# Hybrid trunk, one core: weights of four units split again in the second half, transfers issued one a slot, score groups in pairs

## The reference, cut to what matters

```
h = rmsnorm(x, g_pre[l]) * (1.0 + scale[:, None]) + shift[:, None]
p = h @ w_in[l]                       # 2048 x 1024 by 1024 x 8704
(a_in, a_g, b_q, b_f, b_i, b_g, c_x, c_b, c_c, c_g,
 d_q, d_k, d_v, d_g, m_g) = jnp.split(p, IN_OFFSETS, axis=-1)
y_pool = pool_mixer(a_in, ...) * silu(a_g)
y_hgrn = hgrn2_mixer(b_q, b_f, b_i, ...) * silu(b_g)      # gated linear recurrence
y_conv = short_conv_mixer(c_x, c_b, c_c, ...) * silu(c_g)
y_diff = diff_attention(d_q, d_k, d_v, ...) * silu(d_g)   # causal, two softmax maps a head
merged = sum over branches of sigmoid(m_g) * (y_branch @ w_merge_branch)
x = x + gate[:, None] * rmsnorm(merged @ w_out[l], g_post[l])
```

## Time and profile before

| | us |
|---|---|
| median of 3 runs | 2409.23 (2408.41 to 2409.46) |
| the profiled execution | 2409.45 |
| its span, first to last instruction | 2407.7 |
| TensorE busy | 2245.6 |
| VectorE, ScalarE, GpSimd busy | 1474.8, 1122.4, 847.1 |
| moved by DMA | 569.99 MB |
| mean granted TensorE clock | 0.972 |

### The profile page before, as it was taken

One profiled execution on the slowest core, in us unless ns is written; L12 is line 12 of the kernel. 1 busy time (PEld: TensorE's weight loads), 2 busy tenths in 40 slices (PEclk: granted clock), 3 DMA queues, 4 the chain that ended last, 5 costly groups with the idle time before them and its releaser, 6 DMA issues. The chain is left out here.

```text
span 2407.7 us, 35100 instructions
## 1 busy us (share of the span) xinstructions
PE 2245.6 (93%) x11573; PEld 1857.7 (77%) x11573; DVE 1474.8 (61%) x2645; ACT 1122.4 (47%) x2388; POOL 847.1 (35%) x739
## 2 busy tenths in 40 slices
PE   3798999998999999898999999999999978899998
PEld 3586788887777778786888888878888856787886
DVE  7766777748888795314776666445555435375571
ACT  5543566635454444323656665433434334344351
POOL 1223333326565563101222223133424306363453
PEclk7898999999999999999999999999999989999999
DMA  7899888678877778988565665587877775465561
GB/s 266 297 355 354 285 252 263 233 252 300 271 247 264 253 246 275 345 254 265 160 189 171 171 179 159 169 277 234 248 238 251 219 259 225 146 231 194 186 227 61
DMA packets 340780, 569.99 MB, mean 237 GB/s; under 512 B 27360, under 2 KB 213120, under 8 KB 335744
## 3 DMA queue, kind: packets, MB, share of 16 engines
q1 hardware_dynamic: 306336, 443.04, 54.7%
q10 hardware_dynamic: 34272, 124.80, 16.6%
HBM read 336.53 MB, written 236.45 MB: 238 GB/s over the span
## 5 line engine op out<-in xcount | busy, mean ns | idle before, releaser
L1772 PE MATMUL gb<-h_hi,w_both 128*128 128x512 f32 x1904 | 784.5, 412 | 71.4 <-DVE o L1308 34.1
L1774 PE MATMUL gb<-h_hi,w_both 128*128 128x512 f32 x1904 | 753.8, 396 | 0.0
L1773 PE MATMUL gb<-h_lo,w_both 128*128 128x512 f32 x1904 | 751.6, 395 | 0.0
L1772 PEld LDWEIGHTS gb<-h_hi,w_both 128*128 128x128 f32 x1904 | 363.8, 191 | 155.8 <-issue 79.8
L1774 PEld LDWEIGHTS gb<-h_hi,w_both 128*128 128x128 f32 x1904 | 362.7, 191 | 80.4
L1773 PEld LDWEIGHTS gb<-h_lo,w_both 128*128 128x128 f32 x1904 | 364.9, 192 | 66.2
L999 ACT ACTIVATE o<-gb 128x512 f32<-128x512 f32 x272 | 161.7, 594 | 381.8 <-PE gb L1774 324.8
L863 POOL TENSOR_TENSOR C_prob<-C_prob,C_cf 128x512 f32<-128x512 f32 (+3 forms) x160 | 159.6, 1022 | 464.3 <-DVE C_cf L1416 460.0
L1064 ACT ACTIVATE C_prob<-C_sc,C_negm 128x512 f32<-128x512 f32 (+3 forms) x320 | 198.4, 622 | 223.0 <-DVE C_negm L1394 215.3
L1308 DVE TENSOR_TENSOR o<-gb,o 128x512 f32<-128x512 f32 x204 | 140.2, 688 | 225.8 <-PE gb L1774 205.2
L1298 DVE TENSOR_TENSOR w_both<-w,w_both 128x512 fp32r<-128x512 f32 x170 | 153.3, 902 | 109.8 <-ACT w_both L976 109.6
(11 more groups left out here) (239 smaller groups left out, 3745.0 us busy)
## 6 DMA issues: line engine op xcount, KB each, us to landing
wS_scratch<-w_both SPq DMA_DIRECT2D x238, 512.0 KB, 3.9
w_both<-wS_scratch ACTq DMA_DIRECT2D x238, 512.0 KB, 4.4
w<-in_w_in_dram SPq DMA_DIRECT2D x68, 512.0 KB, 5.4
gT_scratch<-o SPq DMA_DIRECT2D x128, 256.0 KB, 4.6
D_gate<-gT_scratch SPq DMA_DIRECT2D x32, 1024.0 KB, 5.2
pT_scratch<-o SPq DMA_DIRECT2D x80, 256.0 KB, 4.4
D_wm_stage<-wm_scratch SPq DMA_DIRECT2D x32, 640.0 KB, 6.1
C_qt<-qB_scratch SPq DMA_DIRECT2D x128, 128.0 KB, 3.6
```

The lines of the kernel that those rows point to most:

```text
L1772: mm(to, hi[:, k, :], h_hi[j][:, k, :], start=(fresh and k == 0), stop=False, skip_group_check=True)
L1773: mm(to, hi[:, k, :], h_lo[j][:, k, :], start=False, stop=False, skip_group_check=True)
L1774: last = mm(to, lo[:, k, :], h_hi[j][:, k, :], start=False, stop=(k == KH - 1), skip_group_check=True)
```

## The change

- **Weights.** Units 2 to 5 of a half (`REMADE`, products 14 to 41 and 252 to 279) are not stored in the first half and not reloaded in the second. In the second half SP loads their `w1` and `w2` again, and GpSimd, ScalarE and VectorE make sums and splits again. The counts of waits are rewritten for that.
- **Transfers one a slot.** The eight loads of x stand in slots 5 to 12, the operand stores in single slots 19 to 37, and the parts of `begin_attention` become 9 (first half, slots 40 to 48) and 13 (second half, slots 270 to 282) of one load each. The first four staging loads stand two at slot 230 and two at 232.
- **Differences.** The third is made by VectorE at slots 33 and 34, the fourth two slots later; all low parts at `CHANGE` are VectorE's.
- **Scores.** In the second half `rounds` 0 and 1 stand in one slot, 2 and 3 in one slot four later; the picks at offsets 1, 2, 5, 6.

```diff
+REMADE = range(2, 6)
-LOW_BY_VECTOR, LOW_BY_POOL = (0, 2, 3, 6), (1, 4, 5)
-BEGIN = ((39, 2), (279, 1))
+BEGIN = (40, 270)
+def made(n):
+    return n < KEPT or n // PER - NU in REMADE
+def stored(n):
+    return n < KEPT and n // PER not in REMADE
...
+        def score_step(n, r):
+            i = step_in(0, n, 2 * r)
+            return step_in(1, n, (0, 0, 4, 4)[r]) if i is None else i
+        def pick_step(n, r):
+            i = step_in(0, n, 2 * r + 1)
+            return step_in(1, n, (1, 2, 5, 6)[r]) if i is None else i
...
-                if n + LEAD - 1 < KEPT:
+                if stored(n + LEAD - 1):
                     store_weights(n + LEAD - 1)
-                if j == 1 and u + 1 < NU:
+                if j == 1 and made(PER * (u + 1)):
                     load_w1(u + 1)
...
-                    for t in range(8):
-                        load_x(1, t)
+                if PREP <= n < PREP + 8:
+                    load_x(1, n - PREP)
...
                 for half in range(HALVES):
-                    part, odd = divmod(n - BEGIN[half][0], BEGIN[half][1])
-                    if not odd and 0 <= part < 5:
-                        begin_attention(half, part)
+                    if n >= BEGIN[half]:
+                        begin_attention(half, n - BEGIN[half])
...
                 if n == CHANGE[0] - 3:
                     mixers_over(0)
-                    for m in range(STAGES):
+                    for m in range(2):
+                        load_stage(m)
+                if n == CHANGE[0] - 1:
+                    for m in range(2, STAGES):
                         load_stage(m)
...
-                if n + LEAD < KEPT:
-                    high(n + LEAD)
-                elif n + LEAD < PRODUCTS:
-                    load_weights(n + LEAD)
+                if n + LEAD < PRODUCTS:
+                    if made(n + LEAD):
+                        high(n + LEAD)
+                    else:
+                        load_weights(n + LEAD)
...
-                if n + LEAD < KEPT:
+                if n + LEAD < PRODUCTS and made(n + LEAD):
                     low(n + LEAD)
...
                 if n in (PREP + 28, PREP + 29):
-                    t4(1, n - PREP - 28)
+                    t3(1, n - PREP - 28)
+                if n in (PREP + 30, PREP + 31):
+                    t4(1, n - PREP - 30)
...
-                    if n == ATTENTION[half][0]:
+                    if n == BEGIN[half] + 5:
                         begin_attention(half)
...
                 for r in range(4):
-                    i = mix_step(n, 2 * r)
+                    i = score_step(n, r)
                     if i is not None:
                         rounds(i, r)
```

More of the change, by code:

```diff
@@ L80, in column, with in_order, made_before, ring_uses @@
     return PAIR_COLS[u % NU]
+def made(n):
+    return n < KEPT or n // PER - NU in REMADE
+def stored(n):
+    return n < KEPT and n // PER not in REMADE
+def in_order(u):
+    return u if u < NU else u - REMADE[0]
+def made_before(n):
+    return n if n < KEPT else KEPT + sum(map(made, range(KEPT, n)))
+def ring_uses(n):
+    return sum(stored(m) or not made(m) for m in range(n % RING, n, RING))
 def kind(u):
@@ L273, in trunk @@
         w_kept = [sem(f"w_kept{j}") for j in range(RING)]
-        KEEPS = [len(range(r, KEPT, RING)) for r in range(RING)]
         product_done, copied, summed = sem("product_done"), sem("copied"), sem("summed")
@@ L413, in trunk, with step_in @@
         MIX_HALF = NT // 2
+        def step_in(half, slot, offset):
+            i = mix_step(slot, offset)
+            return i if i is not None and i // MIX_HALF == half else None
+        def score_step(n, r):
[4 more added lines that the diff above has]
+            return step_in(1, n, (1, 2, 5, 6)[r]) if i is None else i
         def later(ap, level):
@@ new lines, in _ @@
+                for kk in range(2):
+                    if n == PREP + 14 + kk:
+                        sp.wait_ge(*evicted(1, 2 * kk + 1))
+                        store_operand(0, kk)
+                    if n == PREP + 18 + kk:
+                        sp.wait_ge(*evicted(1, 2 * kk + 5))
+                        store_operand(1, kk)
+                    if n == PREP + 23 + kk:
+                        sp.wait_ge(t1_made, 3 + kk)
+                        store_operand(3, kk)
+                    if n == PREP + 25 + kk:
+                        sp.wait_ge(*evicted(1, 2 * kk + 13))
+                        store_operand(5, kk)
+                    if n == PREP + 27 + kk:
+                        sp.wait_ge(t2_made, 3 + kk)
+                        store_operand(2, kk)
+                    if n == PREP + 29 + kk:
+                        sp.wait_ge(t3_made, 3 + kk)
+                        store_operand(4, kk)
+                    if n == PREP + 31 + kk:
+                        sp.wait_ge(t4_made, 3 + kk)
+                        store_operand(6, kk)
@@ L924, in _ @@
                 u, j = divmod(n, PER)
-                if u + 1 < NU:
+                if made(PER * (u + 1)):
                     if j == 4:
-                        sum_s3_s1(u + 1)
+                        sum_s3_s1(in_order(u + 1))
                     if j == 5:
-                        sum_s2(u + 1)
+                        sum_s2(in_order(u + 1))
                     if j == 6:
-                        sum_s4(u + 1)
-                if n in (PREP + 26, PREP + 27):
-                    t3(n - PREP - 26)
-                for jj, slot in enumerate(CHANGE):
-                    if n == slot and jj in LOW_BY_POOL:
-                        for kk in range(2):
-                            low(jj, kk, stage[(2 * jj + kk) % STAGES])
+                        sum_s4(in_order(u + 1))
                 for half, s in att_slot(n):
@@ L1351, in t2_, with t3 @@
                 tt(parts(t2, kk), parts(h22, kk), parts(h11, kk), ALU.subtract).then_inc(t2_made, 1)
-            def t3_first(kk):
-                dve.wait_ge(t1_made, 2)
+            def t3(half, kk):
+                if half:
+                    dve.wait_ge(*evicted(1, 15))
+                dve.wait_ge(t1_made, 2 * half + 2)
                 tt(parts(h12, kk), parts(h22, kk), parts(h12, kk), ALU.subtract).then_inc(t3_made, 1)
@@ L1626, in _ @@
                     for kk in range(2):
-                        t3_first(kk)
+                        t3(0, kk)
                 if n == 2:
```

113 lines of the change are left out of this document (36 added, 77 removed).

## The result

| | before | after |
|---|---|---|
| median of 4 runs, us | 2409.35 (2408.41 to 2410.76) | 2380.80 (2375.38 to 2384.00) |
| the profiled execution, us | 2409.45 | 2383.72 |
| its span, us | 2407.7 | 2381.9 |

The ratio is 0.9878, with a 95% interval of 0.9859 to 0.9897. The median fell by 28.5 us, where 35.4 were forecast; the profiled execution fell by 25.7.

The account below looks back on a forecast made before the run. Bound by TensorE's work and its waits for copies held up by small stores behind bursts on SP's queue. 6.5 + 15.2 + 0 + 0 + 8.6 + 5.3 = 35.6 us off 2409.45; forecast 2373.8 us, range 2359 to 2389.

Parts of the forecast that it names:

- Slots 31 to 49: First half: nine stores go, bursts are spread and differences move to VectorE; gain 15.2 us (11 to 16.9).
- SP loses at most one landing there: Slot 40, where `begin_attention` waits for the row's store to land; 1.7 us of loss left in slots 31 to 49.
- Slots 5 to 13: First half: loads of x one a slot, stores of products 14 and 15 gone; gain 6.5 us (2.8 to 12.2).
- The 3.1 us that I took for a store in an idle queue: Slots 5 to 13: landing time of a store in an idle queue, taken from about 6.8 us available to land.
- the 3.7 us of slack: Slots 5 to 13: how far the queue may be behind, taking 33.9 us of transfers to 30.2.
- Slots 14 to 30: First half: seventeen more stores (8.9 MB) go where nothing was lost; gain 0.
- Slots 280 to 284: Attention's first loads begin nine slots earlier, where reloads are gone; gain 8.6 of 9.4 us (5 to 9.4).
- Slots 230 to 244 and 245 to 279: Operand change: 0 (3 gained to 5 lost); then 28 reloads become 8 loads, new splits covered three slots ahead: cost 0.
- "slower" rival: Products 252 to 279: every split takes 2.83 us beside GpSimd's sums, 45 us lost, 2418 us; chance 0.02.
- Scores: Second half: joined score groups save entering and leaving, at most 16 x 0.37; gain 5.3 us (3.5 to 5.9).
- the clock rival: Joined score groups: 32 small matmuls taken for a pause, 16 x 1.3 us lost, 5.3 not gained, 2400 us; chance 0.05.
- the queue stays the bound: Gains from bytes alone: 2.8, 11, 5 at attention, 3.5 for scores, 22.3 us in all, so 2387 us; chance 0.14.

Follow-up runs that it names:

- post_early: Changed kernel with the post row's store one slot earlier (slot 38 instead of 39): 2376.86 us.
- both: Changed kernel with the post row's store one slot earlier and units 2 to 6 split again instead of 2 to 5: 2370.84 us.
- x_burst: Changed kernel with the eight loads of x together again in slot 5: 2386.40 us.
- all_reloaded: Changed kernel with no unit split again, all products of the first half stored and reloaded: 2398.86 us.
- late_first_loads: Changed kernel with the first loads of attention's second half again in five bursts at slots 279 to 283: 2388.05 us.
- unit7_too: Changed kernel with the post row's store one slot earlier and units 2 to 7 split again: 2370.34 us.
- unit1_too: Changed kernel with the post row's store one slot earlier and units 1 to 6 split again: 2369.23 us.
- unit6_too: Changed kernel with a fifth unit split again in the second half (units 2 to 6): 2380.61 us.

## Why the prediction came out as it did

**Slots 31 to 49: the term that was mis-sized, 15.2 forecast, 8.8 measured.** The stores left the program as said, but two sentences failed. One was "SP loses at most one landing there", with 1.7 us left for it. SP did lose one landing, 4.4 us, and I didn't ask what is queued behind it: a store of `gS` that ScalarE needs at a fixed moment. post_early shows its price, 3.7 us. The deadline stood in my rows: the 7.43 us that ScalarE waited at 230.78 us are the wait for this same store, in slot 45 of the kernel before, and the change made it 9.77 us instead of removing it. The other was that the stretch's time is bytes by rate. "both" moved 272 GB/s at a share of 0.83 and lost nothing, the changed kernel 292 at 0.84 and lost 8.2 us; what counts is which store is how late against its deadline. With both edits the stretch gained 17.0 us, slightly over my upper end of 16.9.

**Slots 5 to 13: 6.5 forecast, 4.7 measured, by another cause.** I priced the two stores and took them for the least that would be gained. x_burst (37.5 us without them) and all_reloaded (31.9 with them) show that it was the spreading; the two stores are worth less than the scatter. That scatter, 30.2 to 32.4 us for the same code, is a gain of 4.2 to 6.4, so how far 6.5 was off is itself uncertain. The 3.1 us that I took for a store in an idle queue came from a stretch that moved 283 GB/s (500 to 516 us), so it isn't an idle queue's time. The number of the working, 13.79 MB in the stretch, was no given: all_reloaded has the same transfers in these slots, takes 31.9 us and moves 378 GB/s, that is 12.1 MB, because the rest comes in slots 14 to 30. The bytes of a window are what had time to move before it ended. So the sum of bytes by rate and the 3.7 us of slack have no separate measurement: the changed kernel moved 11.9 MB in the stretch at 373 GB/s, 0.8 less than the 12.74 of the working, which is 2.2 us of being behind where I allowed 3.7. By the Trainium skill ("DMA: Bandwidth & Descriptors", Where 436 GB/s comes from) about 358 GB/s is the limit; the rows of 373 to 378, with this one core at work, are above it again.

**Slots 14 to 30: 0, right as a difference, for a reason that I hadn't.** The removed stores are worth 5.3 us there once x is spread (all_reloaded). Had they stayed, that loss would have been new.

**Slots 280 to 284: 8.6 forecast, 9.6 measured.** The place was right; ScalarE's table load is still in slot 284, and nothing shows of the 0.8 us that I left for it. Which part does it was left open; late_first_loads and all_reloaded show that neither does it alone.

**Slots 230 to 244 and 245 to 279: 0 and 0, measured 0.2 gained and 0.** The cover held. The "slower" rival needed every split to be stretched by GpSimd. The splits of `w` from 987.6 to 1086.7 us (min/median/max ns):

```profile
L1313 DVE TENSOR_TENSOR w_both<-w,w_both x20: 691/693/1818, 1000.0 to 1077.2; 128x512 fp32r<-128x512 f32 x20
```

Of all 28 splits there, sums included, four overlapped work of GpSimd, and they took 820, 902, 1683 and 1818 ns; the other 24 overlapped none and took 691 to 694. By the Trainium skill ("GPSIMD Engine Reference", Specifications) the two engines contend for SBUF; the trace shows it in those four. So the rival was wrong on how often the two engines meet, and its 2.83 us a split was too high for the rows here. unit7_too shows where the cover ends, unit1_too that the operand change has none to spare.

**Scores: 5.3 forecast, 5.2 measured** in slots 372 to 468, at clock 1.00 over all of them, so the clock rival is out.

**What was in no term.** Slots 50 to 59 lost 1.2 us: slot 53 took 7.55 instead of 3.70, slot 50 3.89 instead of 5.63. Slot 50 is 3.89 in every kernel that has the change, slot 53 between 3.98 and 7.55. The same code has 45.4 and 46.3 us there in x_burst and late_first_loads, unit6_too and "both" have 44.4 and 44.7, but all_reloaded, with the most bytes before it, has 44.7 as well. So a full queue before doesn't explain it; the cause stays open. The start and slots 0 to 4 were 2.6 us longer and slots 119 to 229 1.3, in code that no kernel here changes; over the traces of the twelve kernels the first product started at 46.6 to 49.0 us, slots 0 to 4 took 33.0 to 35.3 and slots 119 to 229 406.5 to 410.5. That is the scatter of single executions; with slots 50 to 59 and two gains of 1 us each in slots 300 to 371 and behind the start of the last product it leaves some 25.7 us of the 28.5 below. The terms that I named add up to 28.5 in the trace (that the medians also fell by 28.5 is chance), against 35.6 forecast: 6.4 less in slots 31 to 49, 1.8 less in slots 5 to 13, 1.0 more in slots 280 to 284.

The rival "the queue stays the bound" gave 2387, 6.2 us off where the forecast was 7.0 off. Its number is no better founded: it had 2.8 for slots 5 to 13 (4.7 measured, by the spreading), 5 at attention (9.6), and 11 from bytes alone for slots 31 to 49 (8.8).

## What to carry to other kernels

Where an engine waits for a small store, write down for that store when it must have landed and what its queue does before it, waits of the issuing engine included; a stretch's DMA share and its bytes by rate don't tell whether the store is in time. Because the loss begins only past the deadline, two relieving edits can be worth little alone and more than their sum together (0.3 and 3.7 us against 8.2; in slots 266 to 284 2.4 and none against 9.6), so test them together before one is dropped. And a burst that is spread moves its bytes into the next stretch: look whether that one has room (5.3 us here, had the stores stayed).

## What the runs showed of the hardware that I had not expected

- The store of `gS` issued for slot 43 (256 KB) took 6.7 to 7.8 us to land in all four kernels of the table, with 18 MB moved in the stretch or 14.5, though stores of 512 KB took 3.1 in the median of 500 to 516 us, where the core moved 283 GB/s. In front of it stood two loads of `C_ks` and one of `w1` each time, in two of the kernels with a store of weights between; that these alone make the 7 us is my reading and wasn't tried.
- One burst of eight 512 KB loads cost 5.5 us of its stretch (37.5 against 32.0) and bursts of eight `C_ks` and four `C_v_tok` 10.0 (25.7 against 15.7), with the same transfers in the kernel.
- After a wait of TensorE the next slot is slow too: slot 46 took 4.41 to 5.26 us after the waits of slot 45 in the three kernels beside "both" (changed, unit6_too, post_early), and 2.72 in "both". The stretch's granted clock was 0.94, 0.94 and 0.97 there and 1.00 in "both", so part of it ran at 1.2 GHz. In the changed kernel the matmuls from 222.26 to 225.67 us, right after the wait of 6.07 us, started 0.42 to 0.43 us apart and the next ones 0.23, and the clock granted from 218.9 to 223.6 us was 0.50. That makes 1.7 to 2.5 us on top of each wait.
